# A two-block transformer kernel with product-key experts: the first choice of experts made head by head, the row gathers released by the list alone, the sub-keys turned beside the norm, the square-root table loaded early

## What is computed

```python
q = (xc @ w_q).reshape(t, PEER_HEADS, 2, PEER_QDIM // 2)          # 8 heads, 2 halves of 128
sc = jnp.einsum('thpc,hpnc->thpn', q, sub_keys)                    # 128 sub-keys per half
v_half, i_half = lax.top_k(sc, 16)
cand = (v_half[:, :, 0, :, None] + v_half[:, :, 1, None, :]).reshape(t, PEER_HEADS, -1)
top_s, pos = lax.top_k(cand, 16)                                   # 16 experts per head and token
g = jax.nn.softmax(top_s, axis=-1)
u = u_tab[expert]                                                  # 16384 rows of 1024
act = jax.nn.gelu(jnp.einsum('thkd,td->thk', u, xc), approximate=False)
return jnp.einsum('thk,thkd->td', g * act, v_tab[expert])
```

## Time and profile before

| | us |
|---|---|
| median of three runs | 2195.47 |
| the three runs | 2194.08, 2195.47, 2203.77 |
| span of the profiled execution | 2201.1 |
| TensorE, VectorE, ScalarE, GpSimd busy | 1698.5, 1352.4, 390.2, 1172.7 |
| first gather starts at | 575.53 |
| gathered rows, bytes | 1024 gathers, 536.94 MB |
| mean granted TensorE clock | 0.872 |

### The profile page before, as it was taken

How to read it: one execution, slowest core, us unless ns; L and a number is a source line. 1 busy time by engine, 2 the same in 40 slices (tenths; PEclk the granted TensorE clock), 3 DMA queues, 4 the chain that set the end, 5 groups by cost and what they waited for, 6 DMA issues and landing times.

```text
span 2201.1 us, 15874 instructions
## 1 busy us (share of the span) xinstructions
PE 1698.5 (77%) x4674; PEld 869.6 (40%) x4674; DVE 1352.4 (61%) x3251; ACT 390.2 (18%) x912; POOL 1172.7 (53%) x1028
## 2 busy tenths in 40 slices
PE   3997999988456788985876878768678976666665
PEld 1475887445223333432343333324334432222222
DVE  6554431133799684796757578755865985555553
ACT  1022000013011122312122212112222221011011
POOL 0000000000477677676767767765877787777774
PEclk9977999996778968997787999988779999888888
DMA  9841655292799999998999999999999999999996
GB/s 348 309 164 58 198 178 178 67 320 78 267 375 320 401 400 387 401 405 297 397 395 408 403 404 406 379 369 402 398 338 402 409 348 385 387 353 379 371 367 246
DMA packets 254482, 720.79 MB, mean 327 GB/s; under 512 B 24518, under 2 KB 49598, under 8 KB 253886
## 3 DMA queue, kind: packets, MB, share of 16 engines
q0 software_dynamic: 147456, 536.94, 63.5%
q1 hardware_dynamic: 106942, 182.85, 23.3%
HBM read 718.66 MB, written 1.05 MB: 327 GB/s over the span
## 4 chain that ended last, share of the span: by engine, by line
PE 42%; POOL 21%; DMA 13%; DVE 12%; issue 10%; ACT 1%; SPq 0%; another core or an unknown queue 0%; DVEq 0%; ACTq 0%; POOLq 0%
POOL gring L1613 21%; PE PS L594 14%; DMA gring<-in_peer_v_dram,sel_idx 8%; PE PS L706 7%; PE PS L776 6%; PE PS L777 6%; DVE gring L1459 3%; PE PS L533 3%; PE PS L679 2%; DMA gring<-in_peer_u_dram,sel_idx 2%; DMA wring<-in_hyb_w_in_dram 2%; PE PS L643 1%; DVE xs L1477 1%; PE PS L660 1%; DMA gains<-in_g_pre_mix_dram 1%
## 5 line engine op out<-in xcount | busy, mean ns | idle before, releaser
L1613 POOL DMA_INDIRECT gring<-in_peer_u_dram,sel_idx x512 | 581.3, 1135 | 763.3 <-DVE sel_g L1452 575.1
L1459 DVE CUSTOM_DVE_ANT_0 gring<-gring,hs 128x1024 f32<-128x1024 f32 x512 | 618.6, 1222 | 274.3 <-DMA gring<-in_peer_u_dram,sel_idx 243.6
L776 PE MATMUL PS<-gring,diags 128*128 128x512 f32 x768 | 468.9, 696 | 346.8 <-DMA gring<-in_peer_v_dram,sel_idx 156.1
L1613 POOL DMA_INDIRECT gring<-in_peer_v_dram,sel_idx x512 | 591.2, 1155 | 239.3 <-issue 135.0
L777 PE MATMUL PS<-gring,diags 128*128 128x512 f32 x768 | 446.2, 666 | 0.0
L594 PE MATMUL PS<-wring,hTs 128*128 128x512 f32 (+3 forms) x968 | 415.6, 580 | 23.9 <-DMA wring<-in_hyb_w_in_dram 11.3
L776 PEld LDWEIGHTS PS<-gring,diags 128*128 128x128 f32 x768 | 147.6, 214 | 562.9 <-issue 416.9
L594 PEld LDWEIGHTS PS<-wring,hTs 128*128 128x128 f32 x968 | 181.7, 198 | 238.0 <-issue 231.3
L777 PEld LDWEIGHTS PS<-gring,diags 128*128 128x128 f32 x768 | 165.5, 216 | 221.4 <-issue 221.4
L1004 ACT ACTIVATE diags<-consts,acts 128x128 f32<-128x128 f32 x384 | 142.7, 397 | 573.1 <-PE PS L777 372.1
L1477 DVE SCALAR_TENSOR_TENSOR xs<-gring,acts,xs 128x1024 f32<-128x1024 f32 x128 | 164.1, 1282 | 34.8 <-DMA gring<-in_peer_v_dram,sel_idx 31.4
(11 more groups left out here) (182 smaller groups left out, 1116.4 us busy)
## 6 DMA issues: line engine op xcount, KB each, us to landing
wring<-in_peer_w_q_dram SPq DMA_DIRECT2D x32, 1024.0 KB
wring<-in_w_ada_dram SPq DMA_DIRECT2D x24, 1024.0 KB
wring<-in_w_up_dram SPq DMA_DIRECT2D x44, 512.0 KB
wring<-in_hyb_w_in_dram SPq DMA_DIRECT2D x20, 1024.0 KB
wring<-in_w_in_dram SPq DMA_DIRECT2D x10, 1024.0 KB
wring<-in_w_down_dram SPq DMA_DIRECT2D x10, 1024.0 KB
wring<-in_hyb_w_out_dram SPq DMA_DIRECT2D x8, 1024.0 KB
gring<-in_peer_u_dram,sel_idx POOLq DMA_INDIRECT x512
```

Of the source, the lines that this page charges most:

```text
L776: pe.e.matmul(ybank[0], d, row[i % NG][:, 0:512], start=first, stop=last)
L1459: e.tensor_tensor_reduce(row[i % NG], row[i % NG], h[t], 1.0, 0.0, ALU.mult, ALU.add, acts[:, c:c + 1]).then_inc(dotted, 1)
L1613: gp.e.indirect_dma_start(out=row[i % NG], out_offset=None, in_=table, in_offset=bass.IndirectOffsetOnAxis(ap=sel_idx[:, c:c + 1], axis=0) ...
```

## The change

For tile 0 of layer 0 alone, the first pair of heads is chosen as two single heads. So the first choice multiplies by 256 columns instead of 512, and its pick has half the columns and half the instructions in most places; `choose(0, 0)` then has five choices (1, 1, 2, 2, 2 heads). The other three `choose` are unchanged. The units of the single-head steps are halved (`share`). PACE is not touched.

A new semaphore `listed` is raised by the write of `sel_idx`; the gathers wait for it. `gate` still waits for `chosen`.

In `choose(0, 0)` alone the step `keys` moves ahead of `norm`, and a step `warm` (a square root of one column on ScalarE, which brings the table in) is put ahead of `sq`.

```diff
+    "wq1": (D, [(0, 256), (256, 256), (512, 512), (1024, 512), (1536, 512)]),
...
+def choices(t, l):
+
+    return [(0, 1), (1, 1), (2, 2), (4, 2), (6, 2)] if (t, l) == (0, 0) else [(0, 2), (2, 2), (4, 2), (6, 2)]
...
     def choose(t, l):
+        if (t, l) == (0, 0):
+            put("warm")
         put("sq", f"c{t}{l}")
+        if (t, l) == (0, 0):
+            put("keys", t, l)
         yield 2.0
         put("norm", f"c{t}{l}")
...
-        put("keys", t, l)
-
-        def pick(g):
+        if (t, l) != (0, 0):
+            put("keys", t, l)
+        wq = "wq1" if (t, l) == (0, 0) else "wq"
+
+        def pick(g, share):
             for part, units in enumerate((3.0, 3.0, 2.5, 2.5, 2.5, 2.5, 0.5)):
                 put("pick", t, l, g, part)
-                yield units
+                yield share * units
...
-        for g in range(4):
+        for g, (_, heads) in enumerate(choices(t, l)):
+            share = 0.5 * heads
             for k0 in (0, 4):
-                put("mm", ("wq", t, l), (t,), g, k0, t)
-                yield 3.4
+                put("mm", (wq, t, l), (t,), g, k0, t)
+                yield 3.4 * share
                 for _, units in zip(range(4), picking):
                     yield units
             put("qturn", t, l, g)
-            picking = pick(g)
+            picking = pick(g, share)
...
-                cflat = cm.rearrange("p (h c) -> p h c", h=2)
+                cflat = cm.rearrange("p (h c) -> p h c", h=nh)
...
-                    for i in range(2):
+                    for i in range(nh):
                         done(e.max(top[:, i, 0:8], cflat[:, i, :]))
...
-                    done(e.tensor_copy(sel_idx[:, ic:ic + 32], ef[:, 0:32]))
+                    e.tensor_copy(sel_idx[:, ic:ic + m], ef[:, 0:m]).then_inc(listed, 1)
...
-                ve.wait_ge(chosen, chosen_n[(t, l, hd // 2)])
+                ve.wait_ge(chosen, chosen_n[(t, l, choice_of(t, l, hd))])
...
-                gp.wait_ge(chosen, chosen_n[(t, l, hd // 2)])
+                gp.wait_ge(listed, chosen_n[(t, l, choice_of(t, l, hd))])
```

More of the change, by code:

```diff
@@ L45, with choice_of @@
 ROUNDS = [(l, tile, hd) for l in range(2) for tile in range(2) for hd in range(8)]
+def choices(t, l):
+    return [(0, 1), (1, 1), (2, 2), (4, 2), (6, 2)] if (t, l) == (0, 0) else [(0, 2), (2, 2), (4, 2), (6, 2)]
+def choice_of(t, l, hd):
+    return next(g for g, (first, n) in enumerate(choices(t, l)) if first <= hd < first + n)
 def order():
@@ L499, in unit_blocks, with wq_of @@
             return (t + 1) * (3 if name[0] == "a1" else 1)
+        def wq_of(t, l):
+            return ("wq1" if (t, l) == (0, 0) else "wq", t, l)
         def h_groups(name):
@@ L583, in mm @@
                     for tl in tiles:
-                        take(("mm", name, c, tl), "act" if name[0] == "wq" else "vec" if name[0] in (
+                        take(("mm", name, c, tl), "act" if name[0] in ("wq", "wq1") else "vec" if name[0] in (
                             "hyo", "mlo") or name[0] == "hyi" and c < 6 else None)
@@ L1369, in pick @@
             def pick(t, l, g, part):
+                hd0, nh = choices(t, l)[g]
                 b = use[("pick", t, l, g)][0]
-                sc = [PS[:, 512 * b + 128 * j:512 * b + 128 * j + 128] for j in range(4)]
-                ks = [4 * g + j for j in range(4)]
-                cm = work[:, 512 * g:512 * g + 512]
-                cflat = cm.rearrange("p (h c) -> p h c", h=2)
[L1375 to L1383, removed]
+                sc = [PS[:, 512 * b + 128 * j:512 * b + 128 * j + 128] for j in range(2 * nh)]
+                ks = [2 * hd0 + j for j in range(2 * nh)]
+                cm = work[:, 256 * hd0:256 * (hd0 + nh)]
+                cflat = cm.rearrange("p (h c) -> p h c", h=nh)
+                tf = work[:, 4608 + 32 * hd0:4608 + 32 * (hd0 + nh)]
+                tfh = tf.rearrange("p (h t k) -> p h t k", h=nh, t=2)
+                top = work[:, 4864 + 16 * hd0:4864 + 16 * (hd0 + nh)].rearrange("p (h k) -> p h k", h=nh)
+                pos = work[:, 4992 + 16 * hd0:4992 + 16 * (hd0 + nh)].bitcast(U32)
+                posh = pos.rearrange("p (h k) -> p h k", h=nh)
+                ct = ctm[:, 0:256 * nh].rearrange("p (h c) -> p h c", h=nh)
+                ic = 128 * t + 16 * hd0
+                ga = sel_g[:, ic:ic + 16 * nh].rearrange("p (h k) -> p h k", h=nh)
+                s8 = small[:, 352 + 2 * hd0:352 + 2 * (hd0 + nh)]
+                w, o = 32 * nh, 2048 + 256 * hd0
+                pp, pf, ee, ef = (work[:, o + w * q:o + w * q + w] for q in range(4))
                 pp = pp.bitcast(U32)
+                m = 16 * nh
                 if part == 0:
@@ L1391, in pick @@
                         done(e.max_index(ti[:, i, 0:8], tv[:, i, 0:8], s))
-                    for i, s in zip(ks[:3], sc):
+                    for i, s in zip(ks[:-1], sc):
                         done(e.match_replace(tmp[:, i % 4, :], tv[:, i, 0:8], s, LOW))
-                    freed(("pick", t, l, g), e.match_replace(tmp[:, ks[3] % 4, :], tv[:, ks[3], 0:8], sc[3], LOW))
+                    freed(("pick", t, l, g),
+                          e.match_replace(tmp[:, ks[-1] % 4, :], tv[:, ks[-1], 0:8], sc[-1], LOW))
                 elif part == 1:
```

80 lines of the change are left out of this document (42 added, 38 removed).

## The result

| | before | after |
|---|---|---|
| median, us | 2197.14 (20 runs, 2186.28 to 2207.26) | 2207.24 (20 runs, 2195.48 to 2217.83) |
| profiled execution: own time, span | 2203.77, 2201.1 | 2200.21, 2198.3 |
| first gather starts at | 575.53 | 561.25 |
| GpSimd's stall at the end of the first stage | 8.29 | 20.20 |

The ratio is 1.0047, 95% interval [1.003, 1.0064]: the kernel after takes 10 us more. So they are read for where time goes, and the sizes come from the many runs. (The text ahead of the prediction takes the span, 2201.1 us, for that execution's own time; the time is 2203.77 us.)

The account below looks back on a forecast made before the run. The prediction took a serial head of 575.5 us, then transfers in one hardly resting queue, as the bound. Its terms, -11.8 + 1.3 + 8.2 = -2.3 us, made the median 2195.5 into 2193, own range -8 to +2 us, overall 2179 to 2204.

Parts of the forecast that it names:

- The head: Serial chain up to the first gather: savings summing to 16.35 us, first gather at about 559 us.
- the table load: Square-root table load at 539.21 us in the head: run behind earlier copies instead, 1.3 us saved.
- from the norm to the start of the product: In the head: sub-keys turned during the norm wait save 2.7 us, a higher clock for the turns 0.8.
- with 256 columns I take half, 3.5 saved: First product in the head: 16 instructions taking 7.04 us at 512 columns would take half, 3.5 us saved.
- Gather 17: Behind the first gather: waits for the second list, 28.6 us behind the first; costed at nothing, at most 4 us.
- VectorE's stretch: From the first dot to 692 us: VectorE is the bound, gets 20.5 us more work and ends 4.2 us later.
- The net progress: Behind the head: 16.0 us of rows fetched ahead less 4.2 of lateness, 11.8 us, less 1.3 for weights.
- The hole: End of the first stage: slow steps without dots grow, GpSimd's stall goes from 8.3 to 19 us, cost 8.2.
- a stretch that reads so is paced by the transfers: From 695 to 996 us, DMA share 1.02: transfers set the pace, so what starts the stretch earlier ends it earlier.
- rival two: From 695 to 996 us slow steps pace the stage, rows ahead are worth nothing: 2199.7 us, or 2203.7; chance 0.20.
- Rival three: At the first gather: another wait takes its place and it does not move, +12.7 us, 2208; chance 0.03.
- The rest: From 1020 us on: both lists are the same, transfers pace them, and the shift goes through to the end.

Follow-up runs that it names:

- e7: Kernel after with slow steps at their old places between the expert steps and the sub-keys turned at their old place; 2193.17 us, ratio to before 0.9977.
- e11: Kernel before, unchanged, profiled again on a chip where before takes 2154.74 us; 2142.27 us in one run.
- e14: Kernel before with 15.05 empty units put ahead of the hybrid mixer, on a chip where before takes 2155.64 us; 2160.26 us, ratio 1.0031.
- e12_after: Kernel after, unchanged, profiled again on a chip where before takes 2154.74 us; 2150.93 us in one run.
- e13: Kernel after, unchanged, timed in full again on a chip where before takes 2155.64 us; 2158.92 us, ratio to before 1.001.
- e17: Kernel after, unchanged, timed in full a third time, on a slower chip; 2207.58 us, ratio to before 1.0039.
- kept: Kernel after with slow steps at their old places between the expert steps, run three times; 2191.74, 2152.44 and 2195.09 us, ratios 0.9983, 0.9997 and 0.9981.
- e1_pace: Kernel after with PACE[0] at 311.05 instead of 296; 2197.73 us, ratio to before 1.0022.
- e3: Kernel before with 15.05 empty units put ahead of the hybrid mixer, on a slower chip; 2210.52 us, ratio 1.0081.
- e2: Kernel after with slow steps at their old places between the expert steps, first run; 2191.74 us, ratio to before 0.9983.
- e18: Kernel after with slow steps at their old places between the expert steps, third run, slower chip; 2195.09 us, ratio to before 0.9981.

## Why the prediction was wrong, point by point

**The head: 12.98 us between the two profiles, 11.6 against a usual execution of before, not 16.35.** By the chain, from the last residual: the table load 1.28 (forecast 1.3); from the norm to the start of the product 3.22 (2.7 + 0.8); from there to the pick 1.80 (3.5 + 0.45 + 0.8 = 4.75); the pick 6.15 (6.3); the wait for the list 0.53 (0.5). The mis-sized term is "with 256 columns I take half, 3.5 saved". It measured 7.04 to 6.33, 0.7. I had the clock as a gain of 0.8 for the turns and did not ask at which level the product would then run; e7 shows it at 3.62, with the keys back. The product did start earlier, by the 3.22, and what the keys gave there it took back: with the keys at their old place the head is as short (25.10 against 25.29). And 1.35 of the 3.22 is the chance of the first profile, whose 24 turns took 5.38 us where e11 and e14 took 4.2. The further drain of 1.38 us that the Trainium skill (ScalarE: Activation LUTs, What ACT_TABLE_LOAD costs) counts to each table switch is not seen: the stretch with the load shrank by 1.28.

**Behind the head.** Gather 17 came 30.6 us behind the first (forecast 28.6), with a stall of 8.3. VectorE's stretch ended at 702 and not at 700 (695.9 + 4.2). The net progress of 11.8 - 1.3 = 10.5 us is what e12_after has over e11_before on one chip: 11.6 at 820, 10.4 at 960. Against the first profile of before the kernel after has 15.5 at 820, against e11_before 10.8. Right in size by e11_before, and in part by luck: the saving in the head that went into it was too large by 3.4 to 4.7 us.

**The hole.** Stall 20.2 (forecast 19), cost 8.4 us in the kernel after and 5.2 and 5.3 in e12 and e13 (forecast 8.2). By e11_before it is 7.8 in the kernel after and 8.1 in e17. Right, rather high on Q1 and Q2.

**The step that failed** is the one between them: that from 695 to 996 us "a stretch that reads so is paced by the transfers", so that 16.0 us of rows fetched ahead are kept. It is rival two's direction, and the sign I had named for it, rests of the DMA between 695 and 990, is what the trace shows. The forecast put this loss at nothing. In the profile after 10.1 us of lead go there, in e17 7 (12.1 and 9.2 when both stand against e11_before), in e12 and e13 1.2 and 2. Put into the sum, -2.3 + 7 to 10 gives +5 to +8, and with the 12.1 and 9.2 +7 to +10; measured were +10 and +8.5. On Q2, without that loss, +3.3 was measured where the sum says -2.3, though its interval reaches to -4.5. The profile of e13 there is still 4.1 us ahead of e11_before at 1320, so the rest is chance or lies behind 1320; it stays unexplained.

Two other figures of the prediction come near the measured 2207 and are no hits. Rival three's 2208 needs a first gather that does not move; it moved by 14.3 us. Rival two priced the stage at 2199.7 with the hole unchanged; with the 8.2 of the hole added it would be 2207.9. That is its direction and its sign, but it blamed the slow steps alone, and in e12_after the same order of steps keeps the transfers at 1.02 and 396 GB/s from 820 to 900 us.

What makes the loss has two halves. That it takes the late place of the slow steps is shown by undoing it: kept -3.6 and -4.0 us. That it goes along with halts of single engines is shown by the traces: 9.7 and 11.5 us more in the attention of the kernel after on the chips that have them, 1.5 to 4 in kept. That the halts cause it is argued, since no run takes them away on one chip. In the table the kernels with the full shift have the longest attention (97 to 104 us), but e1_pace, 9 steps late, has 89.8, so lateness alone doesn't draw longer halts; why the kernel after meets them is open.

**The rest** went as forecast as far as 1320 us: from 1060 to there the lead moves by 1.3 us at most in every run. Behind 1320 that is not shown. On the slower chips leads of single executions over the first profile of before change by some 9 us either way until 2100 (e7 from 10.3 to 0.9, e3 from -9.2 to -0.7).

## What to carry to other kernels

Where a planner spreads steps by units, a shorter prologue changes the sum of units behind it, and so the place of every later step: rescale so that the places stay, and time that first. Here, on the slower chips, the unscaled weave turned a gain of some 4 us (e2 and e18, each interval touching 1) into a loss of 8 to 10; on Q2 the two stand 6.5 us apart. A step moved into an engine's idle time has to be priced with the clock at which the next one will then run. When a stage reads as paced by transfers, don't book a lead as kept until another order of the same steps has kept it. And one profile is one execution: others of the same kernel showed 1.35 us of the head to be chance, and perhaps 6 us of the lead.

## What the runs showed of the hardware

- The same kernel takes 2155 us on two chips and 2195 to 2199 on the others. From 1900 to 2100 us the transfers move 409 GB/s there in e11_before, 373 in the profile of before. One profile on Q2 (e14_shift, 372 GB/s from 1900 to 2080) has the lower rate with no halts labelled in it, so rate and halts don't always go together.
- On the slower chips engines stand for some 4 to 5 us with nothing to wait for, at the same instruction in two executions (VectorE 4.74 and 4.07 us). All 12 profiles of these chips have "remote" waits of 2 us and more between 560 and 1320 us, the 8 of Q1 and Q2 none. Their cause is open. The packets of the instruction queues (39 of 16 KB and 47 of 8 KB in the page) don't give one: around the halt of VectorE the next one is recorded some 3 us behind the instruction with the halt and without it.
- The label "issue" is no evidence of a halt by itself. ScalarE's waits of 4.13, 4.03 and 3.53 us so labelled in the kernel after are waits of the same length for VectorE in e12_after. Only the length at the same instruction tells.
- TensorE idle for 3.08 us before the turns of h, and then mostly at 1.2 GHz through 24 instructions and 8.5 us (mean granted clock 0.60): a product of 256 columns, 16 instructions, took 6.32 us against 3.62.
- The clock does not come back at the same instruction each time: over the same 24 turns behind the same idle time of 6.11 us it was 0.50 in the first profile of before (5.38 us) and 0.66 in e11_before (4.19 us) and in e3_shift, which ran on a slower chip too.
